# Turning keys and softmax weights on TensorE: from transpose mode to plain fp32 products

## What is computed

```
s = einsum('bqgrd,bgqkd->bgrqk', q_b, keys) * scale - slopes * dist
p = masked_softmax(s, dist >= 0)
o = einsum('bgrqk,bgqkd->bqgrd', p, values)
```

## Time and profile before

| | |
|---|---|
| device time, 3 runs | 1859.77, 1862.10, 1862.11 us; median 1862.1 |
| the profiled execution | 1868.41 us, span of its records 1866.5 us |
| mixed attention stage, in the profiled execution | about 1290 to 1545 us |
| mean granted TensorE clock, share of full | 0.911 over the span |

### The profile page before, as it was taken

One profiled execution on the slowest core, in us unless ns is written; L12 is line 12 of the kernel. 1 busy time (PEld: TensorE's weight loads), 2 busy tenths in 40 slices (PEclk: granted clock), 3 DMA queues, 4 the chain that ended last, 5 costly groups with the idle time before them and its releaser, 6 DMA issues. The chain is left out here.

```text
span 1866.5 us, 37337 instructions
## 1 busy us (share of the span) xinstructions
PE 1639.2 (88%) x13560; PEld 1361.7 (73%) x13560; DVE 901.9 (48%) x1580; ACT 771.8 (41%) x1574; POOL 188.0 (10%) x396
## 2 busy tenths in 40 slices
PE   4899939999999999889899997978777777899996
PEld 3899927665566556559899996976555557799996
DVE  2776166344434444362656633322565643565632
ACT  2666232334433444342454523323454442555521
POOL 0232000110111111100000000021111100000000
PEclk7899966998999999979999998976878877899998
DMA  7244241133312332145355655553343423355640
GB/s 183 92 157 145 68 129 32 42 86 87 84 54 72 89 85 65 52 112 140 100 144 148 177 134 127 158 189 102 119 151 104 146 65 112 91 138 155 173 124 28
DMA packets 283020, 208.15 MB, mean 112 GB/s; under 512 B 29087, under 2 KB 274751, under 8 KB 282448
## 3 DMA queue, kind: packets, MB, share of 16 engines
q1 hardware_dynamic: 273606, 174.22, 33.5%
q0 software_dynamic: 9248, 31.80, 5.4%
q10 hardware_dynamic: 42, 0.44, 0.1%
HBM read 183.57 MB, written 22.85 MB: 111 GB/s over the span
## 5 line engine op out<-in xcount | busy, mean ns | idle before, releaser
L510 PE MATMUL psum<-h_rounded,weights_low 128*128 128x320 f32 x1248 | 393.8, 316 | 30.0 <-DVE h_low_nsa L421 10.2
L510 PEld LDWEIGHTS psum<-h_rounded,weights_low 128*128 128x128 f32 x1248 | 236.2, 189 | 36.4 <-DVE h_low_nsa L421 10.7
L951 PE MATMUL psum<-sbuf_resident 128*128 128x504 f32 x512 | 248.8, 600 | 0.0
L512 PE MATMUL psum<-h_rounded,weights_high_wide 128*128 128x320 f32 x704 | 219.7, 312 | 0.0
L511 PE MATMUL psum<-h_low_ffn,weights_high_wide 128*128 128x320 f32 x704 | 218.4, 310 | 0.0
L512 PE MATMUL psum<-h_rounded,weights_high 128*128 128x320 f32 x544 | 167.6, 308 | 0.0
L585 DVE SCALAR_TENSOR_TENSOR sbuf_stages<-sbuf_stages,sbuf_resident 128x344 f32<-128x344 f32 (+1 forms) x184 | 105.5, 574 | 110.1 <-ACT sbuf_stages L567 106.3
L486 DVE TENSOR_TENSOR weights_low<-sbuf_resident,weights_high_wide 128x2048 fp32r<-128x2048 f32 (+1 forms) x60 | 149.6, 2499 | 14.5 <-ACT weights_high_wide L471 14.5
L471 ACT CAST weights_high_wide<-sbuf_resident 128x2048 fp32r<-128x2048 f32 (+1 forms) x60 | 123.6, 2064 | 59.9 <-DMA sbuf_resident<-in_ffn_w_down_dram 59.9
L984 ACT COPY sbuf_resident<-psum 64x256 f32<-64x256 f32 x256 | 93.8, 367 | 128.2 <-PE psum L944 125.6
L486 DVE TENSOR_TENSOR weights_low<-sbuf_resident,weights_high 128x2048 fp32r<-128x2048 f32 x46 | 105.1, 2292 | 83.4 <-ACT weights_high L471 83.4
(11 more groups left out here) (410 smaller groups left out, 3127.9 us busy)
## 6 DMA issues: line engine op xcount, KB each, us to landing
sbuf_resident<-in_ffn_w_up_dram SPq DMA_DIRECT2D x88, 512.0 KB, 4.8
sbuf_resident<-in_gdn_w_in_dram SPq DMA_DIRECT2D x48, 512.0 KB, 4.7
sbuf_resident<-in_ffn_w_down_dram SPq DMA_DIRECT2D x32, 704.0 KB, 5.9
sbuf_resident<-in_cache_nsa_kv_dram SPq DMA_DIRECT2D x256, 64.0 KB
sbuf_stages<-in_state_gdn_s_dram POOLq DMA_DIRECT2D x16, 512.0 KB, 5.6
out_gdn_s_sample_dram<-sbuf_stages SPq DMA_DIRECT2D x16, 512.0 KB, 3.7
sbuf_resident<-in_gdn_w_out_dram SPq DMA_DIRECT2D x16, 512.0 KB, 5.7
sbuf_stages<-in_cache_nsa_kv_dram POOLq DMA_DIRECT2D x64, 128.0 KB, 3.5
```

What stands on the lines that cost most here:

```text
L510: pe.matmul(out, w_lo, x_hi_tile, start=first, stop=False)
L512: return pe.matmul(out, w_hi, x_hi_tile, start=False, stop=last)
L951: last = pe.matmul(psum[:, H_BANK[t], 0:4 * NC2], w1[:, v, 8 * half + m, t * P:(t + 1) * P], blocks, start=(m == 0 and half == 0), stop=(m ...
```

## The change

Three lines, for three kinds of turn: `pe.transpose(out, in_, ident)` becomes `pe.matmul(out, in_, ident, start=True, stop=True)`. It is the same stationary operand, the same moving identity, the same output and the same semaphores, but an ordinary fp32 product in place of the transpose mode. In each iteration that is 24 key turns (six sets of four; the last iteration has none, the six sets ahead of the loop are changed too), 4 turns of window weights and 8 of selected weights: 36. The other turns (lines 2000, 2084, 2085, 2093, 2094, 2131, 2148) stay in transpose mode. No instruction is added, removed or moved on any engine.

```diff
--- before.py
+++ after.py
@@ -1981,7 +1981,7 @@
                 for j in range(4):
                     src = k_sel[:, 4 * (n % 2) + j, :] if n < 4 else k_win[:, j, :]
                     gp = n // 2 if n < 4 else n - 4
-                    last = pe.transpose(psum[:, b, j * P:(j + 1) * P], src[:, gp * P:(gp + 1) * P], ident)
+                    last = pe.matmul(psum[:, b, j * P:(j + 1) * P], src[:, gp * P:(gp + 1) * P], ident, start=True, stop=True)
                 last.then_inc(A["pe"].sem, A["pe"].step(f"t{n}"))
 
             def act_turn_keys(act, n, it, first=False):
@@ -2073,7 +2073,7 @@
                     pe_compressed_scores(pe, it)
                 pe.wait_ge(as_.sem, as_.count("ewin", i))
                 for j in range(4):
-                    done = pe.transpose(psum[:, X_BANK[2], j * P:(j + 1) * P], sw[:, j * P:(j + 1) * P], ident)
+                    done = pe.matmul(psum[:, X_BANK[2], j * P:(j + 1) * P], sw[:, j * P:(j + 1) * P], ident, start=True, stop=True)
                 done.then_inc(ps.sem, ps.step("ptw"))
 
                 pe.wait_ge(as_.sem, as_.count("ea", i))
@@ -2088,7 +2088,7 @@
                 pe.wait_ge(as_.sem, as_.count("esel", i))
                 pe.wait_ge(ds.sem, ds.count("oT1", i - 1))
                 for j in range(8):
-                    done = pe.transpose(psum[:, X_BANK[j // 4], (j % 4) * P:(j % 4 + 1) * P], ss[:, j * P:(j + 1) * P], ident)
+                    done = pe.matmul(psum[:, X_BANK[j // 4], (j % 4) * P:(j % 4 + 1) * P], ss[:, j * P:(j + 1) * P], ident, start=True, stop=True)
                 done.then_inc(ps.sem, ps.step("pts"))
                 pe.transpose(psum[0:TS, Z_BANK, 0:P], ss[:, PAST:], ident)
                 pe.transpose(psum[0:TS, Z_BANK, P:2 * P], sw[:, WIN:], ident).then_inc(ps.sem, ps.step("ptn"))
```

## The result

| | before | after |
|---|---|---|
| median of 4 runs, us | 1862.1 (1859.8 to 1869.7) | 1907.8 (1902.6 to 1910.9) |
| profiled execution: span, us | 1866.5 | 1900.6 |
| MATMUL records on TensorE, and as many of LDWEIGHTS | 13560 | 13848 |
| mixed attention stage, us | 253.0 | 286.8 |

The ratio is 1.0235, with a 95% interval of 1.0198 to 1.0272. The prediction was 1865.2, in a range of 1859.0 to 1871.5: wrong, and by far.

A forecast was written before the change was run, and what follows sets the result against it. No engine is full; the mixed attention stage is a chain of engines waiting for each other. Exposed loads, 1.9 + 1.2 = 3.1 us, on 1868.4 give 1871.5; less 6.3 to the median, 1865.2 us, range 1859 to 1871.5.

The forecast's parts named there:

- in a run at the full level eight products take 1.05 us: Lines 1029 and 1072, read as 111 ns from product to product, the same as a turn.
- The signs that I had named for a right forecast: Changed lines: durations 275 and 421 ns, firsts 377 and 577, distances 111 and 213; stage about 3 us longer.
- Its own rule for the price: Mixed attention stage: exposed sets on the path times 0.055 us (full level) or 0.10 (half level), 3.1 us in all.
- 19 and 21 exposed sets: 40 sets on the path, loop and ahead of it: 19 begin at half level (1.9 us), 21 at full (1.2 us).
- pts: Turns of selected weights, started after a wait for the exponents; counted as an exposed set on the path.
- t3: Key set right behind the prompt turns; on the path, but its load hidden, so only 0.01 us longer.
- t1, ptw, t3, t4 and t5: Key sets and window weights' turns (ptw) in an iteration, all read as on the path; all but t3 counted as exposed.
- t2: Key set ahead of the next scores; 0.7 us of cover, so its longer load costs about nothing.
- the three exposed ones: About three key sets ahead of the loop, counted among the 40 exposed sets on the path.
- 30 us for an iteration at full clock: Estimate for a loop iteration, against a mean of 31.8 us; gave 13 us less over seven iterations.
- plain products take more passes than I read: Rival: identity products take twice the distance, 288 x 0.11 = 32 us at most on top, 1890; chance 0.02.
- The clock rises: Rival: turns do not count for the clock gate but products do, so the stage speeds up, 1852 us; chance 0.08.

The follow-up runs named there:

- the fillers: 46 unread identity transposes an iteration put ahead of TensorE's waits, added to the kernel before (1856.6 us, 0.9935) and to the change (1876.8 us, 1.0045).
- the keys alone: Only the key turns (line 1984) made plain fp32 products, weights' turns left as transposes, against the kernel before: 1907.2 us, ratio 1.0185.
- two reorders: Kernel before with ScalarE copying tb ahead of t3's copy, and t1 and t5 turned into bank 0: ratio 0.9954; with 40 identity turns an iteration 1843.0 us, 0.9871.

## Why the prediction was wrong

- **The step that failed** is "in a run at the full level eight products take 1.05 us". They were eight records. Line 1072, and the like line 1029, issue two products for each of two heads or operands:

```
for c0, n in chunk[:2]:
    last = pe.matmul(psum[:, A_BANK[h], c0:c0 + n], d["at"][:, c0:c0 + P], d["X"][:, c0:c0 + n], start=True, stop=True)
```

  so x8 in the earlier trace rows is four products. A product takes 223 ns at the full level and 427 at the half level, a turn 109 to 111 and 213. The source and the count stood side by side, and I compared only durations. The turns on line 1984 gave x168 for 42 sets of four, one record each; the same division on line 1072 would have given two. The signs that I had named for a right forecast could not catch this: durations, first durations and distances all came as written, since each of them is that of a record. Only the stage's length was left to speak.
- **Its own rule for the price was near.** With 0.50 and 0.95 us for a set of four in place of 0.055 and 0.10, the same 19 and 21 exposed sets give 18 + 10.5 = 28.6 us. pts has eight turns: eight times 0.45 more at the full level, 3.6. t3 was taken at nothing since its load was hidden; its records are not: 7 x 0.50 to 7 x 0.95, 3.5 to 6.7. In all 36 to 39 us, where the medians give 46 and 40 (1907.8 - 1862.1; 1909.3 - 1868.8), the ratios 44 and 37, and the trace 39. The count of exposed sets held: in an iteration at the full level t1, ptw, t3, t4 and t5 at 0.50 and pts at 0.95 are about 3.4 us, and 3.2 was measured. That t2 is covered was shown. The sets ahead of the loop cost more than the three exposed ones that I had counted (at most 3 x 0.95): 5.3 us, and 4.3 with filled waits. And 30 us for an iteration at full clock, an estimate there, came as 30.0. The rival with the lowest chance, "plain products take more passes than I read", had the mechanism, 288 x 0.11 = 32 us; I gave it 0.02. The 1890 beside it is a slip, 1862.1 and 32 are 1894. Its price was low because it took the full level's distance for all and left out that the stage's clock is at half for a third of the time.
- **The Trainium skill** was right where I argued against it. FP8 and Floating Point Precision, section TensorE Precision Notes, has true fp32 at four passes. 223 ns for 128 columns are 4.2 times 128 periods of 2.4 GHz, and in the trace they come as two records. What Perfetto Trace Analysis, section Transposes, says holds as well: here the transpose takes half the time.
- **"The clock rises"** was rightly put low. The mean clock did not move (0.83 and 0.83). The ground against it, that turns raise the clock, is now shown and not only read: the fillers are transposes, and they lifted the stage from 0.83 to 0.92. The Trainium skill, TensorE: Matmul & The Clock Gate, Part 4, has it that the gate does not engage for transpose mode. For these fp32 transposes that does not hold.
- **What no part of the prediction had:** how much of the price is the clock's. The change costs 37 to 46 us in a stage that is at the half level for a third of its time. With waits filled in both kernels it costs 20 us (1876.8 - 1856.6), about what the same sets give at the full level throughout (40 x 0.50 = 20, with pts and t3 up to 27). So about half of its cost goes when the clock stays up; that it is the added records running at half speed, and not the waits that moved, is argued.
- **Shown and only argued.** Shown: two records to a product (counts), their number as most of the cost (transposes issued twice), the cover of t2, the price of an iteration at the full level, and that filled waits raise the clock and shorten the stage. Argued: the split of the change's 46 us over single sets. Open: why rounded one-record products let the clock fall, and why the keys alone cost as much as they did.

## What to carry to other kernels

Before two kinds of instruction are compared by a group's row, divide its count by the number that the source issues: a duration is that of a record, and an fp32 product here is two. Turn fp32 data with a transpose; a product with the identity takes twice the time of TensorE. In a stage whose mean clock is well below full, price every added record at the level where it runs, and try useless transposes in TensorE's waits: here 334 of them made the kernel 0.65% faster, and with two reorders, which alone gave 0.5%, it came to 1.3%.

## What the runs showed that I had not expected

- A plain fp32 product 128x128x128: at the full level two loads of 186 to 192 ns and two matmuls of 275 ns. The records start 111 ns apart at the full level, 213 at the half.
- Useless transposes raise the granted clock: half-level time of 86 us fell to 38 in the kernel before, of 96 to 10 in the change, of 79 to 21 in the reordered one.
- Products on rounded operands, one record each, doubled the half-level time (86 to 171 us) at an unchanged number of instructions:

```profile
L2093 PEld LDWEIGHTS psum<-ident_rounded,weights_selected_rounded x64: 186/333/338, 1301.5 to 1549.5; 128*128 128x128 f32 x64
L2093 PE MATMUL psum<-ident_rounded,weights_selected_rounded x64: 272/415/471, 1301.5 to 1549.6; 128*128 128x128 f32 x64
```

  Most of these ran at the half level, as the medians of 333 and 415 ns show. The change, which has more records, kept 0.83.
